# Combine the dilated groups and run the sample's dilated attention in one block, with two buffers of sample keys and values

## What is computed

```python
def combine_groups(outs, lses):
    wts = jax.nn.softmax(jnp.stack(lses, axis=0), axis=0).astype(outs[0].dtype)
    o = jnp.einsum('gbsh,gbshe->bshe', wts, jnp.stack(outs, axis=0))
    return o.reshape(o.shape[:2] + (DIL_OUT,))
```

```python
def dilated_sample(q, k, v, buf, span, dilation):
    ...
    kk = jnp.concatenate([buf[:, :, 0], k], axis=1)
    vv = jnp.concatenate([buf[:, :, 1], v], axis=1)
    idx = n_buf + jnp.arange(s)[:, None] - dilation * jnp.arange(span + 1)[None, :]
    ...
    sc = jnp.einsum('bqhe,bqjhe->bhqj', q, kg).astype(jnp.float32) * e ** -0.5
    ...
    o = jnp.einsum('bhqj,bqjhe->bqhe', p, vg)
    return o, jnp.transpose(lse, (0, 2, 1))
```

## Time and profile before

| | us |
|---|---|
| median of 3 executions | 4696.61 |
| lowest and highest of them | 4676.15, 4712.76 |
| the profiled execution, whole | 4696.18 |
| its span in the trace | 4694.3 |

### The profile page before, as it was taken

How to read it: one execution, slowest core, us unless ns; L and a number is a source line. 1 busy time by engine, 2 the same in 40 slices (tenths; PEclk the granted TensorE clock), 3 DMA queues, 4 the chain that set the end, 5 groups by cost and what they waited for, 6 DMA issues and landing times.

```text
span 4694.3 us, 43835 instructions
## 1 busy us (share of the span) xinstructions
PE 3954.0 (84%) x14714; PEld 2589.0 (55%) x14714; DVE 2763.5 (59%) x6631; ACT 1118.9 (24%) x2991; POOL 881.5 (19%) x731
## 2 busy tenths in 40 slices
PE   6789879999981899976998777779998999899983
PEld 5457357888871788843554344434444544444442
DVE  1465434352435111347877999746679766967685
ACT  1346432332331011122222334321111111111111
POOL 0000000101000000001223322233343433334332
PEclk8889869897895699987999778899999999999996
DMA  4000100303115110234888777899999999999994
GB/s 144 4 3 1 52 36 21 129 30 111 49 40 193 43 41 32 105 103 183 312 311 313 286 283 299 311 400 405 404 399 359 407 403 395 368 397 405 404 360 159
DMA packets 286396, 1021.05 MB, mean 218 GB/s; under 512 B 121626, under 2 KB 131250, under 8 KB 201186
## 3 DMA queue, kind: packets, MB, share of 16 engines
q0 software_dynamic: 102864, 727.35, 39.6%
q1 hardware_dynamic: 181858, 288.92, 17.6%
q10 hardware_dynamic: 1456, 2.04, 0.1%
HBM read 968.97 MB, written 49.25 MB: 217 GB/s over the span
## 4 chain that ended last, share of the span: by engine, by line
PE 23%; DMA 17%; DVE 13%; issue 1%; ACT 1%; POOL 0%; SPq 0%; DVEq 0%; ACTq 0%
DMA ff_room<-in_v 11%; PE banks L2251 6%; PE banks L2237 6%; PE banks L2226 5%; DVE ff_rows L1953 3%; PE banks L2180 3%; DMA h<-gates_dram 2%; PE banks L2125 2%; DMA gates_dram<-ff_room 2%; DVE ff_acc L1921 1%; DVE h L1977 1%; DMA ff_rows<-in_uv,pk_expert 1%; DVE h L1982 1%; DVE pk_cand L1645 1%; DVE pk_cand L1648 1%
## 5 line engine op out<-in xcount | busy, mean ns | idle before, releaser
L1857 POOL DMA_INDIRECT ff_rows<-in_uv,pk_expert x640 | 811.5, 1268 | 1609.7 <-DVE ff_acc L1921 782.4
L1953 DVE CUSTOM_DVE_ANT_0 ff_rows<-ff_rows,ff_h_row 128x1024 f32<-128x1024 f32 x648 | 766.9, 1219 | 73.6 <-DMA ff_rows<-in_uv,pk_expert 71.8
L2251 PE MATMUL banks<-ff_room,h 128*128 128x512 f32 x1536 | 706.4, 611 | 74.4 <-DVE h L1991 39.7
L2237 PE MATMUL banks<-h,ff_room 128*128 128x384 f32 x2048 | 686.4, 489 | 13.1 <-ACT h L2097 13.1
L2226 PE MATMUL banks<-ff_rows,ff_diag 128*128 128x512 f32 x1024 | 515.3, 652 | 163.7 <-ACT ff_diag L2041 160.2
L2237 PEld LDWEIGHTS banks<-h,ff_room 128*128 128x128 f32 x2048 | 389.9, 191 | 316.3 <-issue 80.6
L2251 PEld LDWEIGHTS banks<-ff_room,h 128*128 128x128 f32 x1536 | 298.5, 196 | 439.4 <-issue 368.1
L1921 DVE SCALAR_TENSOR_TENSOR ff_acc<-ff_rows,ff_a,ff_acc 128x1024 f32<-128x1024 f32 x388 | 498.3, 1284 | 7.2
L2226 PEld LDWEIGHTS banks<-ff_rows,ff_diag 128*128 128x128 f32 x1024 | 206.4, 209 | 415.3 <-issue 224.9
L2030 ACT ACTIVATE ff_gelu<-ff_dots 128x2 f32<-128x2 f32 x324 | 65.5, 202 | 1253.4 <-DVE ff_dots L1953 1253.4
L175 PE MATMUL banks<-d_w_high,h_high 128*128 128x512 f32 (+1 forms) x648 | 274.3, 423 | 30.9 <-DVE d_w_low L182 30.0
(11 more groups left out here) (371 smaller groups left out, 5845.4 us busy)
## 6 DMA issues: line engine op xcount, KB each, us to landing
ff_room<-in_uT SPq DMA_DIRECT2D x128, 512.0 KB, 10.2
ff_room<-in_v SPq DMA_DIRECT2D x128, 512.0 KB, 19.1
gates_dram<-ff_room SPq DMA_DIRECT2D x6, 4096.0 KB, 17.9
h<-gates_dram SPq DMA_DIRECT2D x128, 192.0 KB, 21.5
d_w<-in_w_dil POOLq DMA_DIRECT2D x9, 2048.0 KB, 8.2
d_w<-in_w_ada POOLq DMA_DIRECT2D x32, 512.0 KB, 4.8
ff_room<-in_w_pq SPq DMA_DIRECT2D x32, 512.0 KB, 4.4
ff_rows<-in_uv,pk_expert POOLq DMA_INDIRECT x640, 10.6
```

The lines of the kernel that those rows point to most:

```text
L1857: pool.indirect_dma_start(out=rows[r][:, :], out_offset=None, in_=IN["uv"][:, :], in_offset=bass.IndirectOffsetOnAxis(ap=at, axis=0))\
L1953: ins = dve.tensor_tensor_reduce(rows[r][:, 0:D], rows[r][:, 0:D], h_row[i % 2][:], 1.0, 0.0, ALU.mult, ALU.add, dots[:, B % RB, j:j + 1])
L2237: ins = pe.matmul(SD[:, 0:ND], u[e % 4][:, k, :], hd[:, k, :], start=(k == 0), stop=(k == KD - 1))
L2251: ins = pe.matmul(Y[j][:, half], ad[e % 2][:, j * P:(j + 1) * P], v[e % 4][:, half_rows[half]], start=(e == 0), stop=(e == NK - 1))
```

## The change

The two functions become one, `stage_combine_and_sample`, with one block. On VectorE the work of tile t of the prompt (`weights(t)`, `mix(t)`) is followed by `keys(i)` for the pairs in `after[t]`. With `after[t]` as written the eight tiles are followed by 2, 1, 2, 1, 2, 1, 2 and 1 pairs. SP issues the loads in the same order, and ScalarE does its value copies between the exponential and the output copy of a tile. `kv` and `qb` have two buffers and not three, `y` has one and not two, the scores `sc` lie in the buffer `x[0]`, and the third `V` has 64 rows. The products for the new token's scores (L1415 before) are done after the seventh tile's transposes and not in the tail. The banks are renamed: N0 to N4 are banks 2 to 6, since banks 0 and 1 are the transposes'. What each operation computes, and its shape, is the same.

```diff
-def stage_dilated_combine(c):
+def stage_combine_and_sample(c):
...
+    KROWS = [128, 128, 64]
+    NB = 2
...
+        y = sb("y", [P, GW])
+        kv = [sb(f"kv{i}", [P, 2, 2 * GW]) for i in range(NB)]
+        V = [sb(f"v{g}", [P if g < 2 else KROWS[2], NSA, GW]) for g in range(NG)]
+        qb = [sb(f"qb{i}", [P, 2, GW]) for i in range(NB)]
...
+        sc = x[0][0:R, 0, 0:NG * (P + NSA)].rearrange("p (g k) -> p g k", g=NG)
...
+        pairs = [(g, b) for g in range(NG) for b in range(0, NSA, 2)]
+        after = {t: [i for i in range(len(pairs)) if i * NT // len(pairs) == t] for t in range(NT)}
+        N0, N1, N2, N3, N4 = c.ps[2:7]
         with nc.Block() as block:
             @block.sync
             def _(sp):
+                sp.dma_start(diag[:], IN["diag"][0:R]).then_inc(s["mask"], 16)
                 for t in range(NT):
                     if t >= 2:
                         sp.wait_ge(s["y"], t - 1)
                     sp.dma_start(x[t % 2][:], c.dram["o_group"][:, t * P:(t + 1) * P, :]
                                  .rearrange("g p w -> p g w")).then_inc(x_in[t % 2], 16)
+                    for i in after[t]:
+                        g, b = pairs[i]
+                        if i >= NB:
+                            sp.wait_ge(s["kT"], i - NB + 1)
+                            sp.wait_ge(s["vv"], i - NB + 1)
+                        n, step = KROWS[g], GROUPS[g][1]
+                        src = IN[f"state{g}"][b:b + 2, 0:step * (n - 1) + 1:step, :].rearrange("b p f -> p b f")
+                        sp.dma_start(kv[i % NB][0:n], src).then_inc(kv_in[i % NB], 16)
+                        q = c.dram["q_dil_sample"][g, b * GW:(b + 2) * GW].unsqueeze(0).to_broadcast([n, 2 * GW])
+                        sp.dma_start(qb[i % NB][0:n].rearrange("p b f -> p (b f)"), q).then_inc(kv_in[i % NB], 16)
...
             @block.vector
             def _(dve):
-                for t in range(NT):
+                def weights(t):
...
-                    if t >= 2:
-                        dve.wait_ge(s["turn"], t - 1)
-                    Y = y[t % 2]
+
+                def mix(t):
+                    X, Y = x[t % 2], y
+                    if t:
+                        dve.wait_ge(s["turn"], t)
...
+                def keys(i):
+                    g, b = pairs[i]
+                    n = KROWS[g]
+                    dve.wait_ge(kv_in[i % NB], 32 * (i // NB + 1))
+                    q = qb[i % NB][0:n]
+                    c.vstep(dve, dve.tensor_tensor(q, kv[i % NB][0:n, :, 0:GW], q, ALU.mult))
+                    dve.tensor_reduce(sT[0:n, g, :, b:b + 2], q.rearrange("p b (h e) -> p h b e", e=DE),
+                                      AX.X, ALU.add).then_inc(s["kT"], 1)
...
+                for t in range(NT):
+                    weights(t)
+                    mix(t)
+                    for i in after[t]:
+                        keys(i)
...
             @block.scalar
             def _(act):
                 for t in range(NT):
                     act.wait_ge(s["diff"], t + 1)
                     act.activation(e[:], e[:], ACT.Exp).then_inc(s["exp"], 1)
+                    for i in after[t]:
+                        g, b = pairs[i]
+                        n = KROWS[g]
+                        act.wait_ge(kv_in[i % NB], 32 * (i // NB + 1))
+                        act.activation(V[g][0:n, b:b + 2, :], kv[i % NB][0:n, :, GW:], ACT.Copy).then_inc(s["vv"], 1)
                     act.wait_ge(s["turn"], t + 1)
...
             @block.tensor
             def _(pe):
...
+                    if t == NT - 2:
+                        pe.wait_ge(s["qz"], 1)
+                        for g in range(NG):
+                            for h in range(DH):
+                                ins = pe.matmul(N1[0:R, g * NSA:(g + 1) * NSA], qz[:, g, h * R:(h + 1) * R],
+                                                c.dks[:, g, h, :], start=(h == 0), stop=(h == DH - 1))
...
```

More of the change, by code:

```diff
@@ L1258, in stage_dilated_combine @@
         m = sb("m", [P, DH])
[L1259 to L1262, removed]
+        y = sb("y", [P, GW])
+        kv = [sb(f"kv{i}", [P, 2, 2 * GW]) for i in range(NB)]
+        V = [sb(f"v{g}", [P if g < 2 else KROWS[2], NSA, GW]) for g in range(NG)]
+        qb = [sb(f"qb{i}", [P, 2, GW]) for i in range(NB)]
+        sT = sb("scoresT", [P, NG, DH, NSA])
+        qz = sb("q_padded", [P, NG, DH * (R + NSA)])
+        diag = sb("diag", [R, NSA])
+        sc = x[0][0:R, 0, 0:NG * (P + NSA)].rearrange("p (g k) -> p g k", g=NG)
+        st = sb("stats", [R, 4])
+        pT = sb("pT", [P, NG, R])
+        pTn = sb("pT_new", [NSA, NG, R])
+        s = {t: c.sem("cs_" + t) for t in ("diff exp y turn copy mask zero kT new nmax s_exp norm pt ptc out qz vv").split()}
+        x_in = [c.sem(f"cs_x_in{i}") for i in range(2)]
+        kv_in = [c.sem(f"cs_kv_in{i}") for i in range(NB)]
+        pairs = [(g, b) for g in range(NG) for b in range(0, NSA, 2)]
+        after = {t: [i for i in range(len(pairs)) if i * NT // len(pairs) == t] for t in range(NT)}
+        N0, N1, N2, N3, N4 = c.ps[2:7]
         with nc.Block() as block:
@@ L1302, in _ @@
                     ins.then_inc(s["y"], 1)
+                def keys(i):
[6 more added lines that the diff above has]
+                                      AX.X, ALU.add).then_inc(s["kT"], 1)
+                c.vstep(dve, dve.memset(qz[:], 0.0))
+                for g in range(NG):
+                    ins = dve.tensor_copy(qz[:, g].rearrange("p (h x) -> p h x", x=R + NSA)[:, :, 0:NSA], c.dqs[:, g])
+                ins.then_inc(s["qz"], 1)
+                dve.wait_ge(s["zero"], 1)
+                for t in range(NT):
[3 more added lines that the diff above has]
+                        keys(i)
+                dve.wait_ge(s["new"], 1)
+                dve.wait_ge(s["mask"], 16)
+                dve.tensor_copy(sc[:, :, 0:P], N0[0:R, 0:NG * P].rearrange("p (g k) -> p g k", k=P))
+                c.vstep(dve, dve.tensor_tensor(
+                    sc[:, :, P:], N1[0:R, 0:NG * NSA].rearrange("p (g k) -> p g k", k=NSA),
+                    diag[:].unsqueeze(1).to_broadcast([R, NG, NSA]), ALU.add))
+                dve.tensor_reduce(st[:, 0:1], sc.rearrange("p g k -> p (g k)"), AX.X, ALU.max, negate=True)\
+                   .then_inc(s["nmax"], 1)
+                dve.wait_ge(s["s_exp"], 1)
+                c.vstep(dve, dve.reciprocal(st[:, 2:3], st[:, 1:2]))
+                dve.tensor_scalar(sc, sc, st[:, 2:3], None, ALU.mult).then_inc(s["norm"], 1)
+                dve.wait_ge(s["out"], 1)
+                dve.tensor_copy(c.o_dilT[:, :, NPR:TOK], N4[:, 0:R].rearrange("p (h b) -> p h b", b=NSA))
             @block.scalar
@@ L1413, in _ @@
-                for g in range(NG):
-                    for h in range(DH):
-                        ins = pe.matmul(c.ps[1][0:R, g * NSA:(g + 1) * NSA], qz[:, g, h * R:(h + 1) * R],
-                                        c.dks[:, g, h, :], start=(h == 0), stop=(h == DH - 1))
+                    ins = pe.transpose(N0[0:R, g * P:(g + 1) * P], sT[:, g].rearrange("p h b -> p (h b)"), c.ident[:, :])
                 ins.then_inc(s["new"], 1)
@@ L1426, in _ @@
                 for h in range(DH):
[L1427 removed]
+                    out = N4[:, h * NSA:(h + 1) * NSA]
                     for g in range(NG):
```

105 lines of the change are left out of this document (18 added, 87 removed).

## The result

| | before | after |
|---|---|---|
| median, us (16 executions each) | 4702.19 | 4664.69 |
| lowest, highest | 4676.15, 4712.76 | 4632.2, 4681.25 |
| profiled execution, us | 4696.18 | 4665.98 |
| its span | 4694.3 | 4663.6 |

The ratio is 0.9919, 95% interval [0.9903, 0.9935]. That is 38 us faster (31 to 46), 0.8%. The forecast was 4665 us, counted from a median before of 4696.61 us (three executions); the sixteen executions put that median at 4702.19.

A forecast was written before the change was run, and what follows sets the result against it. The first function was taken to wait for VectorE, the second for loads. Gains of 29.7 us in the block and 1.4 in the tail took 4696.6 to about 4665 us; likeliest 4650 to 4680, wider range 4644 to 4687.

The forecast's parts named there:

- The first tile: Start of the joined block: VectorE waits 4.6 us for the mask load's issue and the tile's load.
- Eight tiles at 5.00 us: VectorE's prompt tiles: 5.00 us each instead of 6.17, because pairs cover the exponential's wait; 40.0 us in sum.
- Twelve pairs at 2.5 us: VectorE's key operations in the block: two operations and the step between, 30.0 us in sum.
- Waits for loads of 2.3 us: VectorE's waits for loads in the block, between 0 and 17 us possible; last pair then ends at 76.9 us.
- The tail: After the last pair: the new token's products leave this place, a gain of 1.4 us.
- The value products: TensorE's stretch after the tail: stays at 46.2 us, granted clock 0.50.
- The loads as bound: Rival in the block: the load queue sets the pace, gain only 16.4 us, time 4680 us; chance 0.09.
- The slow loop: Rival in the block: two-buffer loop outlasts both old functions, 4706 us at 8 us a pair; chance 0.02.
- The late exponential: Rival in the tiles: ScalarE's value copy holds the exponential, 9.4 us of gain lost, 4674 us; chance 0.05.
- No overlap: Rival in the block: loads and VectorE's work alternate, no gain, time 4695 us; chance 0.03.
- The clock: Rival in the value products: granted clock rises to 1.00, they take half, time 4642 us; chance 0.04.
- The whole: Entire kernel: block and tail together gain 31.1 us, median from 4696.6 to about 4665 us.

The follow-up runs named there:

- e1: Changed kernel with all twelve pairs put behind the eighth tile, without alternation; 4701.75 us, ratio 1.0 to the kernel before.
- e3: Kernel before with ScalarE taking the next tile's exponential ahead of the output copy; 4689.36 us, ratio 0.9977 to the kernel before.
- e8: Changed kernel with repeated queries loaded for the first two pairs only, so output not the reference's; 4681.70 us in a single execution.
- e7: Changed kernel with the new token's 24 products moved back behind the last pair's transposes; 4690.85 us in a single execution.
- e6: Changed kernel with value products turned round: padded probabilities stationary, 512 columns of values moving; 4652.23 us, ratio 0.9886 to the kernel before.
- e5: Changed kernel run again unchanged; 4673.38 us, ratio 0.9919 to the kernel before.
- e2: Changed kernel with one buffer of keys, values and queries instead of two; 4716.13 us, ratio 1.0023 to the kernel before.

## Why the prediction was right, point by point

- **The first tile** was expected at 4.6 us and came at about 4.8 (its first operation waited 3.8 us after the copies of the queries). Right.
- **Eight tiles at 5.00 us.** Right: the wait for the exponential was 0.28 us in each. The runs show why: with the pairs behind the tiles (e1) it is 1.47 us again from the second tile on, with the exponential ahead of the copy (e3) it goes without any alternation. The one `y` cost nothing; no wait for the transposes shows.
- **Twelve pairs at 2.5 us.** Slightly high. Two pairs that follow each other start 2.39 us apart (1456.33 and 1458.72), a little less than their two operations of 1.22 and 1.21 us, since one starts just before the other has ended. Over the twelve pairs that is 0.9 us less: 75.4 less 4.8 for the first tile, 39.9 for eight tiles and 1.6 of waits leaves 29.1 us.
- **Waits for loads of 2.3 us.** 1.6 us for pairs, in pairs 1 and 7 as named. Pair 7 was late again, by 0.94 us and not 1.5; why it is late no run shows, only that the wait goes with the query loads (e8). The sum to the last pair's end was 76.9 and 75.4 was measured: 0.9 us less for the pairs, 0.7 less for the waits, 0.1 less for the tiles and 0.2 more for the first tile. One number of this part was low. The DMA share is 0.88 where near 0.8 was forecast, so the loads kept the DMAs busy for 66 us of the stretch where the sum had 60, and the margin under VectorE's work was thinner than it looked. The mean spacing of 3.84 us that the prediction gives for pairs of 64 rows is the mean of all pairs; the trace bears its conclusion out all the same (last section).
- **The tail** gave 1.4 us, and e7 gives them back.
- **The value products** stayed at 46 us and 0.50, as the trace of before had it and against the rule of the Trainium skill ("TensorE: Matmul & The Clock Gate", Part 1) taken by busy time alone. e6 shows that the clock does rise at this very place for products of 512 columns. These runs don't tell which property of the products decides. (The strip of the page of the kernel before reads 5 and 6 tenths in the slices of the two functions, not 6 and 7 as told at the start; by stretch it is 0.53 and 0.68. Nothing rests on it.)
- **The rivals.** The loads as bound: no (e8), though the margin is thin (e5, e7). The slow loop: with one buffer it does end above the kernel before (e2), so the mechanism is real and the second buffer is what keeps it away. The late exponential: no (its price was 7 x 1.17 = 8.2 us, not 9.4, since the first tile had no late exponential before either). No overlap: no. The clock: no.
- **The whole.** In the trace the block and its tail gave 31.1 + 1.4 = 32.5 us where 29.7 + 1.4 = 31.1 was forecast. The median fell by 37.5 us, interval 31 to 46. That the median of 4664.69 us meets the forecast of 4665 to 0.3 us is luck: it was counted from a median 5.6 us too low, and the gain was larger by about as much. In the profiled execution the 34.7 us from the block's start on, 3.6 more than forecast, are offset by the 4.0 us by which the block started later. The 2.2 us behind the block look like scatter: the next stage's first loads were usable 1.1 us sooner (7.8 us after the first issue and not 8.9), but over all runs this time lies between 7.1 and 8.9 us, in the kernels of either kind. Whether the 5 us between 32.5 and the median's 37.5 are anything but scatter stays open; the scatter ahead of the block is larger than that.

## What to carry to other kernels

Where one stage waits for loads and the next for an engine, put them side by side in units small enough that each covers the other's latency; joining the blocks with two buffers and no alternation gained nothing (e1). Count for each buffer the time from its freeing to its next use and compare it with the load's time from issue to use: 7.3 us against 6.8 was enough, 5.0 and 2.5 were not, and the alternation was worth more than the buffer that it gave up. Look also at the order on the helping engine first: a quarter of this gain was one exponential that stood behind a copy.

## What the runs showed of the hardware

- The loads of pairs of 64 rows kept the DMAs as busy as those of 128 rows, with half the bytes. In the kernel before, 421 GB/s against 207 (columns as in the earlier trace rows):

```profile
1490.20:1501.40 11.20, 0.00 (x0) 0.00 (x0) 7.36 (x7) 3.20 (x4) 0.00 (x0) 0.50 1.03 421
1522.50:1526.30 3.80, 0.00 (x0) 0.00 (x0) 2.43 (x2) 1.06 (x1) 0.00 (x0) 0.50 1.00 207
```

  The pairs nine to eleven became usable 3.5, 3.8 and 3.8 us after the one before, the last after 2.3. Rows 16 apart in the state buffer come with the 64 rows, and no run tells the two apart.
- 192 products of one column, with 24 of eight, kept TensorE busy for 46 us at a granted clock of 0.50 (1.2 GHz) to the end. Products of 512 columns, in the same place, were at 1.00 (2.4 GHz) from 9.5 us on, and their records then started 0.43 us apart and not about 0.87.
- Executions of one kernel lie far apart (4632.2 to 4681.25 us for the changed one). In two traces of the kernel before, the block starts 16.5 us apart, and the granted clock in one stretch far ahead of it was 0.63 in the one and 0.50 in the other. For a change of 30 us in a kernel of 4.7 ms, marks inside the trace tell more than the medians.
